# Channel-form matmuls of an fp32r hybrid decoder layer: one 512-column and one 256-column matmul made into three 256-column matmuls with one sum

## What is computed

```python
h = rms_norm(x, norm1_w[l]) * (1.0 + sc1) + sh1
proj = h @ w_in[l]                       # 2048 x 7168: aq ak av hq hf hi hg
...                                      # dilated attention, HGRN2
x = x + g1 * (y_mix @ w_out[l])
h = rms_norm(x, norm2_w[l]) * (1.0 + sc2) + sh2
u = causal_depthwise_conv(h @ w_up[l], conv_w[l], conv_b[l])   # 2048 x 11264
gate, up = u[..., :D_FF], u[..., D_FF:]
x = x + g2 * ((jax.nn.silu(gate) * up) @ w_down[l])
```

## Time and profile before

| | us |
|---|---|
| median of 3 runs | 1456.58 |
| lowest and highest | 1456.25, 1465.01 |
| span of the profiled execution | 1456.0 |
| PE matmul busy in it | 1280.0 |
| DVE busy in it | 1095.4 |
| ACT busy in it | 579.6 |

### The profile page before, as it was taken

How to read it: one execution, slowest core, us unless ns; L and a number is a source line. 1 busy time by engine, 2 the same in 40 slices (tenths; PEclk the granted TensorE clock), 3 DMA queues, 4 the chain that set the end, 5 groups by cost and what they waited for, 6 DMA issues and landing times.

```text
span 1456.0 us, 20962 instructions
## 1 busy us (share of the span) xinstructions
PE 1280.0 (88%) x6797; PEld 1096.8 (75%) x6797; DVE 1095.4 (75%) x1473; ACT 579.6 (40%) x626; POOL 34.0 (2%) x54
## 2 busy tenths in 40 slices
PE   0118999999997778698799999999999999999995
PEld 0117888888875777487688888888888888888884
DVE  5988997989867897865688888888877776545443
ACT  2104443444441344243454444444444444333342
POOL 3001000000000010000000000000000000000000
PEclk9658999999997899899899999999999999999998
DMA  9886998999952000276287777777766667666662
GB/s 372 351 350 217 398 388 320 369 357 383 368 174 87 0 0 0 87 224 224 106 286 243 231 232 242 233 238 230 229 195 188 189 194 254 196 192 193 196 190 86
DMA packets 136467, 328.11 MB, mean 225 GB/s; under 512 B 9526, under 2 KB 9815, under 8 KB 131427
## 3 DMA queue, kind: packets, MB, share of 16 engines
q1 hardware_dynamic: 134592, 316.71, 64.1%
q0 software_dynamic: 1280, 8.59, 1.6%
q10 hardware_dynamic: 546, 2.20, 0.4%
HBM read 323.26 MB, written 4.19 MB: 225 GB/s over the span
## 4 chain that ended last, share of the span: by engine, by line
PE 82%; DVE 10%; DMA 4%; issue 2%; ACT 2%; DVEq 0%; ACTq 0%; SPq 0%
PE bank L685 33%; PE bank L687 16%; PE bank L709 9%; PE bank L710 9%; PE bank L711 9%; DMA astart<-in_w_ada 3%; DVE acc L913 2%; PE bank L666 1%; DVE msk L1127 1%; DVE proj L1153 1%; PE bank L810 1%; PE bank L760 1%; PE bank L799 1%; ACT junk L516 1%; DVE htmp L972 1%
## 5 line engine op out<-in xcount | busy, mean ns | idle before, releaser
L685 PE MATMUL bank<-h,whi 128*128 128x512 f32 x2048 | 719.3, 397 | 8.1 <-DVE wlo L990 7.3
L990 DVE TENSOR_TENSOR wlo<-wraw,whi 128x1024 fp32r<-128x1024 f32 x404 | 493.7, 1224 | 280.9 <-ACT whi L480 278.8
L480 ACT ACTIVATE whi<-wraw 128x1024 fp32r<-128x1024 f32 x408 | 431.5, 1060 | 608.3 <-PE bank L687 346.6
L687 PE MATMUL bank<-h,wlo 128*128 128x256 f32 x2048 | 572.0, 279 | 0.0
L685 PEld LDWEIGHTS bank<-h,whi 128*128 128x128 f32 x2048 | 386.9, 189 | 99.6 <-DVE wlo L990 8.0
L687 PEld LDWEIGHTS bank<-h,wlo 128*128 128x128 f32 x2048 | 388.1, 190 | 0.0
L709 PE MATMUL bank<-whi,act_hi 128*128 128x512 f32 x352 | 137.0, 389 | 0.3 <-DVE evt L1210 0.3
L711 PE MATMUL bank<-whi,act_lo 128*128 128x512 f32 x352 | 136.9, 389 | 0.0
L710 PE MATMUL bank<-wlo,act_hi 128*128 128x512 f32 x352 | 136.9, 389 | 0.0
L709 PE MATMUL bank<-whi,h 128*128 128x512 f32 x256 | 103.0, 402 | 13.3 <-DVE wlo L990 10.7
L710 PE MATMUL bank<-wlo,h 128*128 128x512 f32 x256 | 102.1, 399 | 0.0
(11 more groups left out here) (196 smaller groups left out, 1024.3 us busy)
## 6 DMA issues: line engine op xcount, KB each, us to landing
wraw<-in_w_up SPq DMA_DIRECT2D x176, 512.0 KB, 3.8
araw<-in_w_ada SPq DMA_DIRECT2D x128, 512.0 KB, 5.8
wraw<-in_w_in SPq DMA_DIRECT2D x112, 512.0 KB, 5.8
wraw<-in_w_down SPq DMA_DIRECT2D x88, 512.0 KB, 4.2
astart<-in_w_ada SPq DMA_DIRECT2D x32, 1024.0 KB, 7.2
wraw<-in_w_out SPq DMA_DIRECT2D x32, 512.0 KB, 3.9
x<-in_x ACTq DMA_DIRECT2D x1, 2048.0 KB, 18.5
x<-in_x POOLq DMA_DIRECT2D x1, 2048.0 KB, 8.6
```

The lines of the kernel that those rows point to most:

```text
L480: act.activation(whi[:, slot], wraw[:, slot], ACT.Copy).then_inc(s_hi, 1)
L685: pe.matmul(out, whi[:, slot, k, cols], h[:, kk].rearrange("p a t -> p (a t)"), start=(kk == 0), stop=False, skip_group_check=True)
L687: last = pe.matmul(out[:, 0:SEQ], wlo[:, slot, k, cols], h[:, kk, 0, :], start=False, stop=(kk == KT - 1), skip_group_check=True)
L990: dve.tensor_tensor(wlo[:, slot], wraw[:, slot], whi[:, slot].bitcast(F32), ALU.subtract).then_inc(s_lo, 1)
```

## The change

In `channel_group`, L685 becomes two matmuls of 256 columns with the same stationary tile of `whi`, the first on the high half of `h`, the second on the low half. Both add into columns 0 to 255 of the bank, where L687 adds too. Nothing is written to columns 256 to 511. ACT copies the finished sums: to `proj` for the first product (`channel_out`), to `evt` for `up`. It raises `s_evac` itself. The adds on DVE (L1003, L1210) and the semaphore `s_evt` go.

```diff
-            def lo_columns(pair, bank0):
-                b = bank0 + 2 * pair
-                act.activation(evt[:, 2 * pair:2 * pair + 2], bank[:, b:b + 2, 256:512], ACT.Copy).then_inc(s_evt, 1)
+            def channel_out(i, ph, pair, tiles_at):
+                b = ph.tile0 % 8 + 2 * pair
+                act.activation(proj[:, bass.ds(i * 4 + (tiles_at + 2 * pair), 2), :], bank[:, b:b + 2, 0:SEQ],
+                               ACT.Copy).then_inc(s_evac, 2)
...
                                     act.wait_ge(s_pe, pe0 + (n - 1 + 2 * pair + 2))
-                                    act.wait_ge(s_evac, i * 4 + (ph.tile0 + 2 * pair - 2 + 4))
-                                    lo_columns(pair, ph.tile0 % 8)
+                                    if pair == 0:
+                                        act.wait_ge(s_evac, i * 4 + (ph.tile0 + 4))
+                                    channel_out(i, ph, pair, tiles_at + 4 * g)
...
-                banks = bank[:, 4 - 4 * half:8 - 4 * half, 256:512]
+                banks = bank[:, 4 - 4 * half:8 - 4 * half, 0:SEQ]
...
-                        act.activation(evt[:], banks, ACT.Copy).then_inc(s_evt, 1)
+                        act.wait_ge(s_pe, pe0)
+                        act.activation(evt[:], banks, ACT.Copy).then_inc(s_evac, 4)
...
-                            pe.matmul(out, whi[:, slot, k, cols], h[:, kk].rearrange("p a t -> p (a t)"),
+                            pe.matmul(out[:, 0:SEQ], whi[:, slot, k, cols], h[:, kk, 0, :],
                                       start=(kk == 0), stop=False, skip_group_check=True)
+                            pe.matmul(out[:, 0:SEQ], whi[:, slot, k, cols], h[:, kk, 1, :],
+                                      start=False, stop=False, skip_group_check=True)
                             last = pe.matmul(out[:, 0:SEQ], wlo[:, slot, k, cols], h[:, kk, 0, :],
...
-                                    if ph.kind == "channel":
-                                        dve.wait_ge(s_evt, i * 2 + (ph.chan0 // 2 + t // 2 + 1))
-                                        dve.tensor_tensor(proj[:, bass.ds(i * 4 + (tiles_at + 4 * g + t), 2), :],
-                                                          bank[:, bank0 + t:bank0 + t + 2, 0:SEQ],
-                                                          evt[:, t:t + 2], ALU.add).then_inc(s_evac, 2)
-                                    else:
+                                    if ph.kind == "token":
+                                        dve.wait_ge(s_evac, i * 2 + (ph.tile0 + 4))
...
-                if step == 0:
-                    dve.wait_ge(s_evt, i * 2 + (chan_groups + half + 1))
-                    dve.tensor_tensor(evt[:], bank[:, 4 * half:4 * half + 4, 0:SEQ], evt[:], ALU.add).then_inc(s_evac, 4)
-                elif step == 1:
+                if step == 1:
```

More of the change, by code:

```diff
@@ L254, in build @@
         s_pe = sem("s_pe")
-        s_evt = sem("s_evt")
         s_evac = sem("s_evac")
@@ L484, in hi_ahead, with stream @@
                 hi_part((unit0 + j) % RING, i * loads + ((unit0 + j) // RING + 1) * 16, slot_free(ph, pe0, j))
-            def lo_columns(pair, bank0):
-                b = bank0 + 2 * pair
-                act.activation(evt[:, 2 * pair:2 * pair + 2], bank[:, b:b + 2, 256:512], ACT.Copy).then_inc(s_evt, 1)
-            def stream(name):
+            def channel_out(i, ph, pair, tiles_at):
+                b = ph.tile0 % 8 + 2 * pair
+                act.activation(proj[:, bass.ds(i * 4 + (tiles_at + 2 * pair), 2), :], bank[:, b:b + 2, 0:SEQ],
+                               ACT.Copy).then_inc(s_evac, 2)
+            def stream(name, tiles_at=0):
                 with act.Fori(0, PH[name].groups // 2) as turn:
                     i = turn * 2
-                    for ph in (PH[name], Group(PH[name], 1)):
+                    for g, ph in enumerate((PH[name], Group(PH[name], 1))):
                         pe0 = i * ph.pe_per + ph.pe0
@@ L539, in _ @@
             h_hi(0)
-            stream("hq_hf")
+            stream("hq_hf", HQ)
             stream("hi")
@@ L544, in _ @@
             act.activation(proj[:, HQ:HQ + 8, :], proj[:, HQ:HQ + 8, :], ACT.Silu).then_inc(s_gates, 1)
-            stream("hg")
+            stream("hg", HG)
             act.activation(proj[:, HF:HF + 8, :], proj[:, HF:HF + 8, :], ACT.Sigmoid).then_inc(s_gates, 1)
-            stream("aq_ak")
+            stream("aq_ak", AQ)
             act.wait_ge(s_evac, PH["aq_ak"].tile0 + 4)
@@ L621, in _ @@
                         act.wait_ge(s_convg, 11)
-                        act.activation(evt[:], bank[:, 4:8, 256:512], ACT.Copy).then_inc(s_evt, 1)
+                        act.wait_ge(s_pe, ph.pe0)
+                        act.activation(evt[:], bank[:, 4:8, 0:SEQ], ACT.Copy).then_inc(s_evac, 4)
                     unit = ph.unit0 + g * ph.units + j
@@ L1198, in _ @@
             ph = PH["up"]
-            chan_groups = ph.chan0 // 4 * 2
             def conv_step(i, half, step):
```

## The result

The changed kernel takes 1477.84 us (1476.23 to 1480.14, 4 runs) against 1456.41 us for the kernel before, a ratio of 1.0124 with a 95% interval of 1.0085 to 1.0163. It is 21.4 us slower, where 26.3 were forecast. The profiled span is 1478.3 us, 22.3 more than before. The 1456.41 is the median of four runs, of which three lie near 1456 us and one at 1465. The kernel before has two paces, and the part on its two rhythms takes this up.

What follows compares the result with a forecast made beforehand. TensorE's matmul stream was taken as the bound, with evacuation, ring and weight transfers ahead of it. 1456.0 + 26.6 - 0.3 = 1482.3 us span, so 1483 us; own range 1476 to 1492, full range 1455 to 1500.

Steps and rivals of the forecast that it cites:

- Step 1: Channel matmuls: a 256-column one costs 0.1201 us, with 0.0135 fixed per matmul, so a triple takes 0.3603 against 0.3468.
- The lower bound: For the 256-column matmul: 0.1125 us, from 16 plain float32 matmuls in 1.80 us; three would take 0.3375, a gain.
- Step 2: Sum over PE's stretches: +21.4 us in `hq_hf` and `up`, 5.2 in `hg` and `aq_ak`, 79 other pairs at nothing; +26.6 together.
- two readings: `hg` and `aq_ak`: triple 0.3603 there too, 2.7 us, or a dearer 256-column matmul kept, 10.2 us; 5.2 was taken.
- Step 3: DVE loses 40.5 us of adds, ACT's copies keep their sizes; only 0.3 us of PE idling before `down` goes, -0.3 us.
- Step 4: Waits and orders of ACT, DVE, banks and transfers: cost nothing and gain nothing; PE's waits in `up` stay as short.
- The cut is free: Rival: 256-column matmuls step at 0.1156 us, three again 0.3468, so 1456 us minus 0.3, within 1%; chance 0.15.
- the lower floor: Rival: three 256-column matmuls in a row run at 0.1125 us each, so the kernel gets faster, 1435 us; chance 0.13.
- Weight loads become the bound: Rival: three loads per triple set the pace; 0.1266 us a step gives 1519 us, 0.1515 some 210 us longer; chance 0.12.

Runs made afterwards that it cites:

- the run with the evacuation alone: Changed kernel with its three matmuls put back to the 512- and 256-column pair, ACT's new copies kept, DVE adding nothing: 1464.05 us, ratio 1.0016 to the kernel before.
- the one with the cut alone: Kernel before with only the 512-column matmul cut into two of 256, each into its own half of the bank, old evacuation kept: 1479.75 us, ratio 1.0129.

## Why the prediction was right

**What bounds the kernel.** Right. TensorE's stream was the bound. DVE at 81 to 93% looked close by, but in the run with the evacuation alone it had 36 us less to do and the pace of the pairs stayed.

**Step 1, the price of a 256-column matmul.** Right: 0.1200 us measured, 0.1201 forecast, and 0.0133 us of fixed cost for 0.0135. The assumption under it, that a 512-column matmul costs in a pair what it costs in `down`, was measured at 0.2267 in a row of such matmuls. In a mixed row single matmuls differ from that, but the two prices add up to the faster rhythm, 0.2267 + 0.1200 = 0.3467. The reading of single starts, on which the rival of a free cut rested, was misleading: in the earlier trace rows the steps are 0.24 and 0.11, while the matmuls cost 0.2267 and 0.1200. The cost isn't one of 512-column matmuls alone, since three of 256 take 0.3600 us where their 768 columns are 0.32. Nor is it one of changing from `whi` to `wlo`, since the cut adds no such change and costs 0.0133.

The lower bound was ill chosen. The 16 matmuls of L815 have 128 columns, and the plain float32 ones of 256 columns are the "neighbour" at 0.215:

```profile
L815 PE MATMUL bank<-msk,hv 128*128 128x128 f32 x128 | 15.6, 275 | 0.0
L827 PE MATMUL bank<-probT,avh 128*128 128x256 f32 x16 | 4.8, 379 | 0.0
```

So 0.1125 is no price for 256 columns. It is close to the 0.112 of fp32r matmuls with 128 columns.

The Trainium skill, "TensorE: Matmul & The Clock Gate", section "Back-to-back issue gap", gives 2.5 ns beyond the columns for an isolated warm matmul. The streams here, in which each matmul has its own weight load, don't follow that: the cut cost 0.0133 us.

**Step 2, the sum.** Right in sign and place, 4.0 us too high in the profiles (26.3 against 22.3). The terms, forecast and measured:

| | forecast | measured |
|---|---|---|
| up to the start of `hg` | 2.9 | 2.1 |
| `hg` and `aq_ak` | 5.2 | 2.6 |
| from there to `up` | 0 | -0.1 |
| `up` | 18.5 | 18.3 |
| behind `up` | -0.3 | -0.5 |

The mis-sized term is `hg` and `aq_ak`. I took the middle of two readings, and the lower one was true: the stages had no dearer 256-column matmul, only the pair had the slower rhythm there, and equal matmuls have no such rhythm. So 384 x (0.3600 - 0.3533) = 2.6 us. The same confusion of a stage with a rhythm hid that the kernel before has two times.

Part of the nearness is luck. The profile that the prediction started from had `up` in the faster rhythm, and three of the four runs lie in the faster heap. In the slower rhythm `up` would have lost 1372 x (0.3600 - 0.3534) = 9.1 us and not 18.3, and nothing in the prediction allowed for that.

The first term has hidden parts. The last 224 pairs of `hq_hf` took 2.9 us more (80.4 and 83.2), as 213 x 0.0133 = 2.8 says. The first channel matmul was late by 0.4, and the 32 pairs of the first stretch, costed at nothing, brought 0.5. But `hi` behind them was shorter by 1.6 us, 50.5 and 48.9, because the clock was at half for less time. The windows of the kernel before, and then of the one after:

```profile
238.50:242.00 3.50, 3.50 (x14) 3.11 (x15) 1.95 (x2) 0.00 (x0) 1.66 (x1) 0.50 0.99 360
242.00:245.30 3.30, 3.30 (x9) 2.62 (x8) 0.00 (x0) 0.00 (x0) 0.63 (x2) 0.50 0.60 230
```

```profile
238.50:242.00 3.50, 3.50 (x29) 3.31 (x27) 3.50 (x5) 1.06 (x1) 0.00 (x0) 1.00 1.02 393
242.80:246.20 3.40, 3.40 (x11) 2.82 (x11) 1.34 (x2) 0.00 (x0) 2.29 (x2) 0.50 0.97 343
```

About 3.4 us less at half clock is 1.7 us less time. Other kernels here show either length of this stretch, or none at all (the clock was 1.00 from 236 to 250 in the run with the evacuation alone). The run with the three matmuls in another order, which has the same matmuls as the changed kernel, had it as long as before (a mean of 0.76 in that window, as before, for 0.88 in the changed kernel). So nothing shows that it is owed to the change.

**Step 3, DVE and ACT.** Right, and a little too small. DVE's busy time fell by 34.8 us, less than the 40.5 of added-up durations. Most of the difference is overlap with the records of neighbouring instructions: in the trace of the kernel before, the adds make up only 36.1 us of DVE's busy time. The idle time in front of `down` is gone. The timeline of the kernel before there, and then the chain of the changed one:

```profile
1196.53 0.28 PE L687 MATMUL bank<-h,wlo 128*128 128x256 f32 x1
...
1200.53 0.47 PE L709 MATMUL bank<-whi,act_hi 128*128 128x512 f32 x1 [0.29 <-DVE evt L1210]
```

```profile
1219.56 0.12 PE bank L692
1219.68 3.44 PE bank L839 x8
1223.11 0.23 PE bank L714
```

From the last matmul of `up` to the first of `down` it is 4.00 us in the kernel before and in the one with the cut alone, and 3.15 in the changed kernel and in the one with the evacuation alone. The records' 0.29 of idle time hid this, as the modelled ends of the eight matmuls ahead reach over the gap. Some 0.3 us goes again in the first step of `down`, 0.63 us long for 0.31, so 0.5 is left.

**Step 4, waits.** Right: PE waits once in `up`, 1.0 us for 1.2 before.

**The rivals.** "The cut is free" and "the lower floor" are out by the triple of 0.3600. "Weight loads become the bound" is out at 256 columns: at 0.1200 a matmul with its load is slower than the 0.112 that shorter ones reach, and far from 0.1515. At 192 columns and below a floor holds, which may be theirs. The Trainium skill, "Perfetto Trace Analysis", section "Identifying the Most-Contended Engine", has TensorE's headroom judged by its weight loads. The direction agrees with the trace, where PEld was at 87% in `up` and is at 100% now. As a size it says less, since the triple grew by 3.8% where the loads grew by half.

**The range.** The upper end of the forecast's own range, 1492, is 3 us more than its terms give, 1456.6 + 21.4 + 10.2 + 1.1 - 0.3 = 1489.

## What to carry to other kernels

On a kernel bound by TensorE count matmuls as well as columns: for fp32r, at 256 and 512 columns and the full clock, each one cost 0.0133 us beyond its columns, so two results that share a stationary tile belong in one wide matmul, and an add on another engine that isn't waited for was the cheaper way to join them. Read the price of a matmul from long rows of starts and from a difference of two rows, not from single steps in a mixed stream. Where a program's runs fall in two heaps, compare the pace of its steady stretches in two profiles of it before costing a change to 1%.

## What the hardware showed that I had not expected

- A stream that alternates 512- and 256-column fp32r matmuls has two rhythms, 0.3467 and 0.3534 us a pair, each stable over hundreds of pairs, and one program took either in `up` in two executions (spans 1456.0 and 1464.6 us). Streams of one length show a single pace: 0.3600 for three of 256 and 0.4533 for two of 512.
- In rows of eight long and eight short ones, the first five 512-column matmuls behind the short ones take 0.228 to 0.236 us and the last three 0.2267, whatever changes of bank and moving tile lie between.
- Matmuls of fewer than 256 columns gain almost nothing: 0.112 us at the full clock with 128 columns, against 0.1200 with 256, and 0.212 us at half the clock.
- With 128-column matmuls the granted clock was 0.50 for a whole stretch from 142 to 285 us in which PE and its loads were recorded as busy all the time; with 256 columns it was at a mean of 0.96 in the same work. This kernel, with far fewer columns, took longer (1513.35 us) than the one with all of them (1477.84).
